# Router logits out of the output projections, the eight-largest instruction for the choice, expert seats filled earlier, and empty slots left out of the gathers

## What is computed

```
x  = x + gate1 * (mixed @ w_out)
h2 = modulate(rms_norm(x, norm_ffn), shift2, scale2)
# block 1: softmax over 4 groups, best group, best 2 of its 8 experts
# block 2: logits = h2 @ router_w + router_b ; best 4 of 32, softmax over the 4
x  = x + gate2 * sum_e combine[:, e] * expert_e(h2)
```

## Time and profile before

| | |
|---|---|
| median of 3 runs | 2654.95 us |
| span of the profiled execution | 2660.2 us |
| TensorE / VectorE / ScalarE / GpSimd busy | 90% / 39% / 18% / 8% |
| block 1: output projection starts, router starts, first turned rows of the experts | 476.1, 552.3, 603.3 us |
| block 2: the same | 1485, 1549.4, 1602.8 us |
| block 1's output projection, one `u` | 8.6 us |
| bytes moved by DMA | 691 MB, 260 GB/s over the span |

### The profile page before, as it was taken

One profiled execution on the slowest core, in us unless ns is written; L12 is line 12 of the kernel. 1 busy time (PEld: TensorE's weight loads), 2 busy tenths in 40 slices (PEclk: granted clock), 3 DMA queues, 4 the chain that ended last, 5 costly groups with the idle time before them and its releaser, 6 DMA issues. The chain is left out here.

```text
span 2660.2 us, 33243 instructions
## 1 busy us (share of the span) xinstructions
PE 2389.1 (90%) x12564; PEld 1149.9 (43%) x12564; DVE 1046.4 (39%) x2301; ACT 490.6 (18%) x1140; POOL 224.5 (8%) x248
## 2 busy tenths in 40 slices
PE   7999878968886899999999968999899999999974
PEld 3444666434443555667544422333233342333323
DVE  4856564751111555458522162223232222222215
ACT  3233531021111311166111021000000000000003
POOL 0000000001101000048400001000000000000002
PEclk9999777879997899899999989999999999999996
DMA  8534403679998600010311067999999999999995
GB/s 341 224 127 150 151 1 112 260 288 363 418 384 350 236 32 3 32 64 1 131 64 63 0 282 302 411 420 416 419 419 393 418 420 419 420 418 419 419 419 185
DMA packets 144197, 691.32 MB, mean 260 GB/s; under 512 B 14908, under 2 KB 42684, under 8 KB 78488
## 3 DMA queue, kind: packets, MB, share of 16 engines
q1 hardware_dynamic: 120920, 635.19, 59.1%
q0 software_dynamic: 9376, 31.73, 3.2%
q10 hardware_dynamic: 13744, 22.30, 2.3%
HBM read 640.14 MB, written 49.02 MB: 259 GB/s over the span
## 5 line engine op out<-in xcount | busy, mean ns | idle before, releaser
L2044 PE MATMUL bank<-ring,ex_xt 128*64 128x512 f32 (+4 forms) x2240 | 364.1, 518 | 25.9 <-DMA ring<-in_up 23.4
L2044 PE MATMUL bank<-x_spare,ex_xt 128*64 128x512 f32 (+4 forms) x1504 | 267.8, 508 | 16.9 <-DMA x_spare<-in_up 16.0
L2044 PEld LDWEIGHTS bank<-ring,ex_xt 128*64 128x64 f32 (+2 forms) x2240 | 129.3, 134 | 243.0 <-issue 194.3
L2085 PE MATMUL bank<-ring,ex_at 128*32 128x256 f32 (+2 forms) x1168 | 191.8, 506 | 10.6 <-DMA ring<-in_down 8.2
L2168 ACT ACTIVATE ex_xt<-bank 128x512 f32<-128x512 f32 (+1 forms) x85 | 42.7, 526 | 830.9 <-PE bank L2025 825.8
L2044 PEld LDWEIGHTS bank<-x_spare,ex_xt 128*64 128x64 f32 (+2 forms) x1504 | 97.1, 133 | 175.2 <-issue 140.6
L1992 POOL DMA_INDIRECT ex_x<-rows,index x74 | 71.1, 961 | 1079.7 <-PE bank L2025 1054.7
L2085 PE MATMUL bank<-x_spare,ex_at 128*64 128x512 f32 (+2 forms) x720 | 136.9, 523 | 14.3 <-DMA x_spare<-in_down 11.8
L2319 DVE COPY ex_y<-bank 128x512 f32<-128x512 f32 (+1 forms) x83 | 48.1, 599 | 250.7 <-PE bank L2085 250.6
L2553 PE MATMUL bank<-hT,ring 128*128 128x512 f32 x320 | 142.5, 599 | 2.5 <-ACT hT L2603 2.5
L2276 DVE TENSOR_TENSOR ex_hb<-bank,ex_bias 128x512 f32<-128x512 f32 x40 | 27.5, 687 | 223.3 <-PE bank L2044 223.3
(11 more groups left out here) (583 smaller groups left out, 3300.8 us busy)
## 6 DMA issues: line engine op xcount, KB each, us to landing
ring<-in_up SPq DMA_DIRECT2D x170, 1024.0 KB, 24.1
x_spare<-in_up SPq DMA_DIRECT2D x120, 1024.0 KB, 27.9
ring<-in_down SPq DMA_DIRECT2D x82, 1024.0 KB, 27.7
x_spare<-in_down SPq DMA_DIRECT2D x64, 1024.0 KB, 24.6
hT<-in_up SPq DMA_DIRECT2D x30, 1024.0 KB, 26.3
ring<-in_w_in SPq DMA_DIRECT2D x14, 2048.0 KB, 12.9
ring<-in_w_ada SPq DMA_DIRECT2D x12, 2048.0 KB, 8.4
ring<-in_w_mod SPq DMA_DIRECT2D x12, 2048.0 KB, 7.6
```

What stands on the lines that cost most here:

```text
L2044: last = nc.tensor.matmul(k.ps[up_bank(b, p, r)][g * rows:(g + 1) * rows, 0:c.stop - c.start], rows_in, w[:, c], start=kk == 0, stop=kk == ...
L2085: last = nc.tensor.matmul(out, rows_in, w[:, g * width:(g + 1) * width], start=f == 0, stop=f == FT - 1)
```

## The change

- `output_phase` now loads the router's weights `w_rt`. GpSimd makes two copies of them: `wg`, scaled by the gain, and `wr`, scaled by the shift. After each part `u` of the residual, TensorE multiplies it (as stationary operand, 128 tokens at a time) by `wg` and adds into one bank: unnormalized logits with tokens on partitions. A product with ones gives the shift's part, which VectorE adds to the bias as `lrow`. The sums of squares are made with tokens on partitions by products with one column; GpSimd adds the squares of parts 1 to 6 to `hT[0]` in both blocks. The full `rn` and its reciprocal leave this phase.
- SyncE issues seat loads in the output projection: `x_spare`'s six seats (that buffer is now shared with the mixer's tiles, whose data is dead by then), and ring halves once their slot has been used: 10 of 16 seats in block 1, 12 in block 2. The router issues the rest.
- `router_phase` takes a 4-column inverse root, multiplies the logits by it, adds `lrow`, and chooses with `max` and `max_index` (the eight largest of a row and their places), one each for 128 tokens; all one-hots come from one comparison. The row scaling moves from VectorE to GpSimd (8 products 128x512), and the turning of `hT` behind the counting products. The group softmax, the weights and `mass` move behind the index; GpSimd issues the first gather at the router's end.
- Slots without a token now get the index of a row out of range, and the gathers have a bounds check that lets them be left out, so that the buffer keeps old rows there.
- `gate2_phase` keeps its tiles in the shared buffer. The rest of that diff is indentation.

```diff
@@ output_phase @@
+        wr, at = carve(room, 0, (KT, n_logits))
+        wg, at = carve(room, at, (KT, n_logits))
+                def seat_load():
+                    to, src, landed, slot = seats.pop(0)
+                    if slot is not None:
+                        sp.wait_ge(k.used[slot], sum(k.slot[i] == slot for i in range(keep)))
+                    sp.dma_start(to, src).then_inc(landed, 16)
+
+                sp.dma_start(wr, w_src).then_inc(s_w, 16)
+                for j in range(NM):
+                    k.send_pieces(sp, mod + j + 1)
+                    if j and seats[0][3] is None:
+                        seat_load()
                 k.send_pieces(sp, keep)
+                while seats:
+                    seat_load()
+                def logits(u):
+                    pe.wait_ge(s_sb, u + 1)
+                    if u == 0:
+                        pe.wait_ge(s_wg, 1)
+                    for i in range(NT):
+                        nc.tensor.matmul(k.ps[5][:, i * 64:i * 64 + n_logits], k.xT[:, u, i * P:(i + 1) * P], wg[:, u, :], start=u == 0 and i == 0, stop=u == KT - 1 and i == NT - 1)
+                def square_sums(u):
+                    for i in range(NT):
+                        nc.tensor.matmul(k.ps[6][:, i:i + 1], k.hT[:, u, i * P:(i + 1) * P], k.c("one"), start=u == 0 and i == 0, stop=u == KT - 1 and i == NT - 1)
-                            if gated is None and u >= 1:
-                                pe.wait_ge(s_sq, u)
-                                nc.tensor.matmul(k.ps[5][:, :], k.c("ones"), k.hT[:, u - 1, :], start=u == 1, stop=False)
+                            if h == halves - 1 and u >= 1:
+                                logits(u - 1)
+                pe.wait_ge(s_ws, 1)
+                for kk in range(KT):
+                    last = nc.tensor.matmul(k.ps[7][:, 64:64 + n_logits], k.c("ones"), wr[:, kk, :], start=kk == 0, stop=kk == KT - 1)
+                last.then_inc(s_row, 1)
+                pe.wait_ge(s_added, KT - 2)
+                square_sums(0)
+                logits(KT - 1)
                 pe.wait_ge(s_sq, KT)
+                square_sums(KT - 1)
+            @block.gpsimd
+            def _(pool):
+                pool.wait_ge(s_w, 16)
+                pool.tensor_tensor(wg, wr, bc(gain, n_logits), ALU.mult).then_inc(s_wg, 1)
+                pool.tensor_tensor(wr, wr, bc(shift, n_logits), ALU.mult).then_inc(s_ws, 1)
+                for u in range(1, KT - 1):
+                    pool.wait_ge(s_sq, u + 1)
+                    pool.tensor_tensor(k.hT[:, 0, :], k.hT[:, 0, :], k.hT[:, u, :], ALU.add).then_inc(s_added, 1)
-                dve.wait_ge(s_rt, 1)
-                dve.reciprocal(k.rn[:], k.rn[:])
+                dve.wait_ge(s_row, 1)
+                dve.tensor_tensor(k.lrow[:, 0:n_logits], k.ps[7][:, 64:64 + n_logits], b_row, ALU.add)
@@ router_phase @@
+                act.activation(rn4[:], k.ps[6][:, 0:NT], ACT.Sqrt, scale=1.0 / D, bias=k.c("eps")).then_inc(s["rms"], 1)
+                for i in range(NT):
+                    act.activation(diag[:, i, :], k.c("ident"), ACT.Copy, scale=rn4[:, i:i + 1]).then_inc(s["diag"], 1)
...
+                act.activation(k.rn[:], k.ps[0][:, :], ACT.Copy).then_inc(s["rn"], 1)
+                lgp = k.ps[5][:, 0:256].rearrange("p (i n) -> p i n", i=NT)[:, :, 0:n_logits]
+                run(dve.tensor_tensor(lg[:], lgp, bc(rn4[:], n_logits), ALU.mult))
+                run(dve.tensor_tensor(lg[:], lg[:], bm(k.lrow[:, 0:n_logits], NT), ALU.add))
+                for i in range(NT):
+                    dve.max(best[:, i, :], choice[:, i, :])
+                for i in range(NT):
+                    dve.max_index(which[:, i, :], best[:, i, :], choice[:, i, :])
+                run(dve.tensor_copy(ek[:], which[:, :, 0:top].rearrange("p i n -> p n i")))
+                run(dve.tensor_tensor(oh_flat, bm(k.c("slot", 0, E), top * NT), bc(flat(ek), E), ALU.is_equal))
-                for n in range(top):
-                    first_max(lm[:], k.c("rev"), m[:, n, :], eq[:], ek[:, n, :], key[:], E)
-                    run(dve.tensor_tensor(oh[:, n], key[:], bc(ek[:, n, :], E), ALU.is_equal))
-                    run(dve.scalar_tensor_tensor(lm[:], oh[:, n], -3.0 * BIG, lm[:], ALU.mult, ALU.add))
+                run(dve.tensor_scalar(whose[:], whose[:], -MAGIC, -1.0, ALU.add, ALU.min))
+            @block.gpsimd
+            def _(pool):
+                pool.wait_ge(s["rn"], 1)
+                for kk in range(KT):
+                    pool.tensor_tensor(k.hT[:, kk, :], k.xT[:, kk, :], k.rn[:], ALU.mult).then_inc(s["scaled"], 1)
                 pool.wait_ge(s["split"], 1)
                 for a in range(OWN, NA):
                     place_token(pool, a).then_inc(s["put"], 1)
+                pool.wait_ge(s["sent"], 16 * NT)
+                pool.wait_ge(s["index"], 1)
+                gather_rows(k, pool, t, plan, 0, plan.parts(0), lambda p: x[:, 0, (512 * p):], x_in[0])
@@ new: gather_rows, used by the router and by expert_phase @@
+        pool.indirect_dma_start(out=to(p)[:, 0:D // groups], out_offset=None, in_=k.a["rows"].rearrange("r (g d) -> (r g) d", g=groups),
+                                in_offset=bass.IndirectOffsetOnAxis(ap=t["index"][:, at_:at_ + 1], axis=0),
+                                bounds_check=T * groups - 1, oob_is_err=False).then_inc(landed, 16)
@@ two_blocks @@
+SPARE = [(i, None) for i in range(8, SEATS - 2)]
+            early, late = seat_loads(seats, PLAN1, a["up1"], a["down1"], k.seat_in["ex1"], SPARE + [(4, 2), (5, 2), (0, 0), (1, 0)])
+            early, late = seat_loads(seats, PLAN2, a["up2"], a["down2"], k.seat_in["ex2"], SPARE + [(4, 2), (5, 2), (6, 3), (7, 3), (0, 0), (1, 0)])
```

More of the change, by code:

```diff
@@ L1447, in attention_phase, with output_phase @@
     k.end()
-def output_phase(k, name, mix, first, halves, gate, keep, mod=None, gated=None):
+def output_phase(k, name, mix, first, halves, gate, keep, early, w_src, n_logits, b_row, gain, shift, room, mod=None, gated=None):
     nc = k.nc
@@ new lines, in _ @@
+                col, split, n = plan.first_col, plan.first_split, plan.count
+                every = lambda ap, first, step, count: ap[:, first:first + step * count].rearrange("p (u o) -> p u o", o=step)
+                dve.drain()
+                many = plan.cols - col["N"]
+                for g in range(4):
+                    rows = slice(g * QUARTER, (g + 1) * QUARTER)
+                    dve.tensor_scalar(t["index"][rows, col["N"]:plan.cols], every(what[rows, :], split["N"], 2, many)[:, :, g % 2], 2.0, float(g // 2), ALU.mult, ALU.add)
@@ L3198, in two_blocks @@
[L3198 to L3206 removed]
+                sb("wr", [P, 2 * KT * (4 + E)])
```

600 lines of the change are left out of this document (293 added, 307 removed).

## The result

The changed kernel took 2636.4 us (median of 4 runs, 2627.5 to 2641.4) beside 2655.4 us of the kernel before (4 runs, 2653.2 to 2656.3): a ratio of 0.993, interval 0.991 to 0.995. Timed again beside the first experiments it gave 2641.8 us (12 runs, 2630.6 to 2648.2) against 2654.8, 0.995 (0.994 to 0.997). So it is faster, by 13 to 19 us, where 48 were forecast; 2607 is too low and the range, which ended at 2626, does not hold the time.

A forecast was written before the change was run, and what follows sets the result against it. Expert stages were taken as bound by weight bytes, their start by VectorE's router chain. Terms -19.7 - 18.6 - 0.8 + 3.4 - 12 = -47.7 from 2660.2 gave 2612.5, or 2607 us for the median; range 2594 to 2626.

The forecast's parts named there:

- The choice, the logits, the map: Routers of blocks 1 and 2: one-hots' sum 6.4 and 4.7 us after the start, digits and map 4.05 and 6.85.
- projection 2: Block 2's output projection: new sum-of-squares products and narrow records make the router start 3.4 us later.
- The skip: Expert stages: leaving out slots without a token moves 3.7 and 2.6 MB less, taken as -12 us.
- Rival 3: Expert stages: checked gathers become the bound in block 1 and the kernel gets slower, near 2697 us; chance 0.06.
- Its last part is issued near 17, and seven us are left: Block 1's router: the token rows' write to HBM has seven us to land before the first gather.
- The first gather is issued beside them and lands within 4 us. Phase boundary 2.2: Router's end: the gather runs beside the group sum and weights, then a 2.2 us boundary to the next stage.
- rival 4: Experts' start: a late seat or the rows' write holds it back, giving back at most 5 to 10 us; no separate chance.
- Rival 2: Routers: GpSimd's eight products hold up VectorE's chain, 8 us a block, 2623 us; chance 0.12.
- rows 8 and 9: Trace rows cited against rival 2: with both engines busy, VectorE and GpSimd both slow down, neither stops for long.
- Warm-up 2.8 us: Router's end: three warm-up products on TensorE take 2.8 us, now on the path instead of hidden behind the gather.
- Projection 1, -0.8: Block 1's output projection: 0.8 us shorter, with 40 records (4.4 us) replacing the root and the 3.35 us reciprocal.
- The seat is issued behind its piece: Block 1's output projection: six 1 MB seat loads among the pieces cost nothing, or 6 us if the cover fails.

The follow-up runs named there:

- free_vector: gather_next with GpSimd's eight row products by the inverse root also left out in both routers (token rows lack that factor): 2620.5 us, ratio 0.988.
- the experiment: Changed kernel with slots without a token fetched again, all with token 0's row: 2649.5 us, ratio 0.998, where the changed kernel had 0.995.
- last_seats: Changed kernel with the loads of the last two seats waiting until the token rows' writes have landed: 2633.5 us, ratio 0.992.
- gather_next: last_seats with the first gather issued at the beginning of the expert stage instead of the router's end: 2625.3 us, ratio 0.989.
- o1_seats: Changed kernel with block 1's six early seat loads issued behind the last modulation piece instead of one behind each: 2632.7 us, ratio 0.991.
- again: Changed kernel unaltered, timed again beside the others: 2641.8 us over 12 runs (2630.6 to 2648.2).
- warm_tail: Changed kernel, shift's logit products ahead of the last modulation columns, six wide products among the narrow ones ending both output projections: 2649.1 us, ratio 0.998.

## Why the prediction missed

The direction and four of its terms were right; the steps marked wrong below failed. The largest is the end of the routers: the write of the token rows and the first gather, which the sum held to be beside the path, were the path.

- **The choice, the logits, the map: right.** One-hots' sum 5.7 and 4.9 us (6.4 and 4.7 forecast), digits and map 4.05 and 6.95 (4.05 and 6.85), projection 2 +4.0 (+3.4). With late rows, gather and GpSimd out of the way the router of block 1 took 31.4 us, and 31.3 was the forecast; block 2's 36.9 against 34.8. That 31.4 meets 31.3 is partly luck: in free_vector VectorE ended at 24.7 us where the sum has 26.25, and barrier and warm-up together took 6.7 instead of 5.0. In block 2 both were above the sum (30.7 for 29.75, 6.1 for 5.0).
- **The skip: right**, 6.0 and 4.4 us by the experiment's stages (7.7 by its median), 11.4 by the stages against before, 12 forecast. Rival 3 did not come: the 15 gathers of block 1's middle land in 6.8 us, 6.9 before.
- **"Its last part is issued near 17, and seven us are left": wrong.** This is the step that failed in the routers, together with the next one. The last part was issued 20 us after the start, GpSimd having been released only at 6.2, and the gather that waits for it started at 32.9, more than 12 us later. The release was late by the clock: the two wide products ahead of the inverse root, two records each, ran at the lower level, 3.75 us, where four such records had taken 1.88 at the upper one in the kernel before (547.4).

```profile
559.03 3.75 PE L372 MATMUL bank<-cst 128*128 128x512 f32 x4 [1.04 <-PEq L320]
```

  The trace of before had the landing. SyncE waited 12.3 us for it there, from 573.2, when its last seat was issued, to 585.5:

```profile
SPq L1596 <- DMA rows<-rt_htok: 12.3, 1, 12.3
```

  That is 16 us after the last part was issued (569.5) and still 10 us before `index` was there (596.1), so nothing waited for it. I looked at the loads and the gathers for durations and not at the write. In the changed kernel it is slow because two seats of 1 MB leave just then: without them beside it, in last_seats, a part lands in 4.9 us instead of 11.1.
- **"The first gather is issued beside them and lands within 4 us. Phase boundary 2.2": wrong.** The edit put a transfer ahead of a barrier, and the barrier followed its landing. I counted it as work beside the path. From VectorE's last instruction to the next stage it took 6.5 and 4.9 us instead of 2.2 each. Taking both this step and the one before it away gave 7.6 us in block 1 and 2.1 in block 2 (gather_next). It is rival 4, which I had at 5 to 10 us, near the 9.7 it costs in all, but as an end of the range and not as a term.
- **Rival 2 came, at chance 0.12, with 3.0 and 4.0 us** instead of 8 a block. My rows 8 and 9 were of long instructions on both sides, where a wait for the other is a fraction of the duration. Here VectorE's instructions last 0.15 us and GpSimd's 1.23, so one that collides can wait for most of one: 1.15 to 1.31 us. Which ones keep their time can be read off: those with an operand in PSUM (L1786, L1793, 0.37 and 0.31 us) and the reduction L1802 in block 2 (0.59 us at 1557.31, beside a product). The Trainium skill ("SBUF — State Buffer", Who interferes with whom) has this as an exclusive lock. A VectorE instruction takes it with two SBUF inputs, against a GpSimd instruction that reads SBUF, or in a two-port mode; a reduction never does on this chip. The trace agrees in each of these rows. But not every instruction from SBUF waits: L1784 and L1789, 1.28 and 1.31 us in block 1, take 0.15 and 0.17 beside the products of block 2. I had weighed the rule as one of price and taken the wrong rows for it.
- **Warm-up 2.8 us: wrong**, 5.25 and 4.2. TensorE had nothing to do while the barrier waited for the gather, 588.5 to 595.8 us; the granted clock was 0.68 in 590 to 595 and 0.50 in 595 to 600. Before, it waited 1.3 us and ran at 1.00. The wait is not all of it: in gather_next it was 1.9 us, and the warm-up still took 4.5, with the clock at 0.50 in 581 to 583.
- **Projection 1, -0.8: wrong, +6.7.** "The seat is issued behind its piece, so I cost it at nothing; if the cover fails, 1 us for each." The cover failed: pieces landed in 9.4 us instead of 7.5. o1_seats gives 3.6 us back (0.8 to 4.7 against the spread of the unchanged projection). "40 records (4.4 us)" was measured at 8.7, for the clock. Together they are more than the 7.5 us, for they overlap: 1.6 of the 3.6 us are a shorter stretch at the lower clock.
- **Two readings were off without a part in the sum.** In the earlier trace rows DMA reaches 9 tenths from slice 25 on, not 24, with 393 GB/s in slice 30. And 384 MB counts an expert as 12 x 1024 x 1024 bytes, where the profile's MB are 1,000,000 bytes: 403 of those at 419 GB/s are 961 us of block 2's 1000, not 916, which makes the case for a stage bound by bytes stronger.

The range erred by taking the misses one at a time. It reached to the costliest rival that it meant to hold, the second, but the late rows, the barrier, GpSimd's products, the clock and the seats are not exclusive, and all five came.

## What to carry to other kernels

When a chain is shortened by 20 us, list what ran hidden beside it and give each its own end time from the trace, issue and landing: the write of 2 MB, the gather, the seats and the boundary were all free under the long chain and became the path together. Issue no transfer ahead of a barrier because "it lands meanwhile" unless the barrier's other side is later anyway; and when an experiment that frees one suspect changes nothing, free the second with it before acquitting either. Putting 1 us instructions on GpSimd beside a chain of 0.15 us ones on VectorE can cost up to one GpSimd instruction for each that reads only SBUF; here eight of them cost 3.0 and 4.0 us. Place them where VectorE reads PSUM, reduces or waits. Before a gain of 2 or 3 us is believed, compare the stage with several profiles of unchanged code: the first projection alone spread over 4 us.

## What the runs showed of the hardware

- Four MAX8 over 32 values take 0.47 us, a FIND_INDEX8 0.18 with 0.07 to 0.09 for loading its values.
- A gather whose entries are out of bounds keeps its packets (2373 against 2370) and moves 4.09 instead of 7.61 MB; the time on the engines follows the bytes.
- A stage's closing barrier came 0.9 to 1.0 us after the landing of the last gather that GpSimd had issued (594.9 to 595.84; 1581.0 to 1581.99; 595.0 to 595.98 in last_seats), and 0.95 us after VectorE's end where no gather was issued (gather_next).
- TensorE's granted clock fell from 1.00 to 0.50 while its records showed it busy all the time, in a stretch of products with 1 to 36 columns (o1_seats, busy in all of 541 to 549 us, fell at 547.9; the run `again`, idle 0.44 us at 542.4, at 545.7), and also just after one 128x512 product among them (warm_tail, at 545.0). Busy time in the records is then no sign that the clock stays. The Trainium skill ("TensorE: Matmul & The Clock Gate", What's actually happening) describes the lower level as the default and the state after idling; in warm_tail TensorE's records leave no idle time in 540 to 550 us.
